# Gate and up projection of a decoder block as seven block products instead of eight, with the sums on VectorE

## What is computed

```python
h = rms_norm(x, norm_mix[l])
proj = h @ w_in[l]                                   # eight streams of 1024
# ... conv branch y_a, pooling branch y_p, cross-attention branch y_x ...
merged = sigmoid(g_a) * y_a + sigmoid(g_p) * y_p + sigmoid(g_x) * y_x
x = x + merged @ w_out[l]

h = rms_norm(x, norm_ffn[l])
x = x + (silu(h @ w_gate[l]) * (h @ w_up[l])) @ w_down[l]
return rms_norm(x, norm_final)
```

## Time and profile before

| | us |
|---|---|
| median of 3 runs | 1152.45 (1149.39 to 1160.99) |
| the profiled execution | 1155.09 |
| its span on the slowest core (core 0) | 1153.5 |
| spans of the other cores | 1144.2 to 1151.8 |
| busy in the span, TensorE / VectorE / ScalarE | 1117.5 / 475.7 / 305.2 |
| granted TensorE clock, mean of core 0 | 0.993 |

### The profile page before, as it was taken

The page is one execution under the profiler, slowest core; times in us unless marked ns, Lnnn a source line. Parts: engine busy times, 40 slices in busy tenths (PEclk is TensorE's granted clock), DMA queues, the critical chain, the costliest instruction groups (busy, mean ns, idle before and its releaser), DMA issues.

```text
span 1153.5 us, 14599 instructions; the slowest of 8 cores (1144.2 to 1153.5 us)
## 1 busy us (share of the span) xinstructions
PE 1117.5 (97%) x5472; PEld 543.1 (47%) x5574; DVE 475.7 (41%) x482; ACT 305.2 (26%) x490; POOL 79.0 (7%) x153
## 2 busy tenths in 40 slices
PE   7998999997999999999999999999999999999998
PEld 3665545553444444444444444444444444444444
DVE  5452555462765654654554632111324221112223
ACT  5432443423212224331212210111522121111111
POOL 1110000100011010001001000211000000000000
PEclk9998999999999999999999999999999999999999
DMA  9999861478387979345226453999966354200132
GB/s 246 173 205 203 148 128 55 80 159 127 74 137 209 258 164 175 67 123 110 56 54 110 74 146 110 204 182 171 172 164 194 101 117 82 40 1 1 37 110 110
DMA packets 78916, 146.34 MB, mean 127 GB/s; under 512 B 46571, under 2 KB 46571, under 8 KB 78592
## 3 DMA queue, kind: packets, MB, share of 16 engines
q0 software_dynamic: 21456, 77.64, 39.6%
q1 hardware_dynamic: 57392, 67.78, 20.2%
HBM read 185.27 MB, written 23.07 MB: 181 GB/s over the span
## 4 chain that ended last, share of the span: by engine, by line
PE 85%; DMA 10%; DVE 2%; issue 2%; ACT 1%; SPq 0%; DVEq 0%; ACTq 0%; POOLq 0%
PE ps L228 85%; DMA ring<-w_in 3%; DMA ring<-w_kv 3%; DMA arena<-hb 3%; DMA arena<-x 1%; ACT tmp L419 1%; DVE tmp L390 0%; SPq L177 0%; DVE tmp L470 0%; DVE smx L416 0%; DVE tmp L383 0%; DVE arena L397 0%; ACT tmp L387 0%; DVE tmp L483 0%; DVE hb L331 0%
## 5 line engine op out<-in xcount | busy, mean ns | idle before, releaser
L228 PE MATMUL ps<-hA,ring 128*128 128x512 bf16 (+3 forms) x2446 | 503.5, 363 | 6.6 <-ACT hA L352 2.5
L228 PEld LDWEIGHTS ps<-hA,ring 128*128 128x128 bf16 x2496 | 243.2, 98 | 259.6 <-issue 5.2
L228 PE MATMUL ps<-arena,ring 128*128 128x512 bf16 (+1 forms) x1575 | 333.3, 369 | 13.1 <-ACT tmp L460 6.1
L228 PEld LDWEIGHTS ps<-arena,ring 128*128 128x128 bf16 x1600 | 158.0, 99 | 184.2 <-issue 14.7
L228 PE MATMUL ps<-arena 128*128 128x512 bf16 (+1 forms) x838 | 180.4, 373 | 0.8
L629 DVE TENSOR_TENSOR arena<-ps,tmp 128x1024 bf16<-128x1024 f32 x44 | 53.9, 1225 | 227.9 <-PE ps L228 224.1
L228 PEld LDWEIGHTS ps<-arena 128*128 128x128 bf16 x854 | 83.6, 98 | 96.3
L625 ACT ACTIVATE tmp<-ps 128x1024 f32<-128x1024 f32 x44 | 45.0, 1023 | 253.4 <-PE ps L228 253.4
L470 DVE TENSOR_TENSOR tmp<-tmp 128x1024 f32<-128x1024 f32 (+6 forms) x40 | 49.2, 1230 | 41.4 <-ACT tmp L460 38.9
L228 PE MATMUL ps<-ring,arena 128*128 128x512 bf16 x250 | 57.4, 379 | 0.6 <-issue 0.2
L218 POOL DMA_DIRECT2D ring<-w_in x48 | 25.6, 538 | 440.0 <-PE ps L228 359.3
(11 more groups left out here) (98 smaller groups left out, 583.6 us busy)
## 6 DMA issues: line engine op xcount, KB each, us to landing
ring<-w_in POOLq DMA_DIRECT2D x48, 512.0 KB, 12.9
ring<-w_gate_up POOLq DMA_DIRECT2D x44, 512.0 KB, 12.2
arena<-x SPq DMA_DIRECT2D x32, 512.0 KB, 6.7
tmp<-x_scr SPq DMA_DIRECT2D x24, 512.0 KB, 5.3
x_scr<-arena SPq DMA_DIRECT2D x16, 512.0 KB, 3.5
out<-tmp SPq DMA_DIRECT2D x15, 512.0 KB, 3.3
arena<-w_down POOLq DMA_DIRECT2D x11, 512.0 KB, 24.3
ring<-w_kv POOLq DMA_DIRECT2D x8, 512.0 KB, 23.1
```

Source lines behind the costliest of these rows:

```text
L228: ins = e.matmul(o, l, r, start=s0, stop=s1)
```

## The change

**The scheme.** For a chunk the gate and up weights are a 2 by 2 block matrix (gate or up; first or second half of the contraction), and so are the tokens (half of the contraction; tokens 0 to 511 or 512 to 1023). The four output blocks come from seven products of four 128x512 matmuls each. For this some products need sums of weight blocks or of token blocks, and the outputs are sums of products.

**Token sums** (`x_sums`): for each of four blocks of 128 tokens five VectorE operations of 512 bf16 columns, into three ring slots that are taken for good (`x_slots`, `slots_held`) and in place in `HA`. For half 0 they are put into merge chunks 4 and 5 of half 1, for half 1 into the down stage of half 0. **Weight sums** (`w_sums`): for each chunk three VectorE operations in bf16, of 1024, 512 and 1024 columns, into `kT` or `vT` (free by then) and in place in the weight's slot. They are issued for chunk `c + 1` in the middle of chunk `c`; for chunk 0 in merge chunk 7, and at the last down tile of half 0.

**The chunk** (`gate_up`): three banks a chunk (A, C, D in the order bA, bC, bD). Bank D and bank A are written, read by VectorE and written again within the chunk; bank D and C also collect two products. The evaluation is 2 copies and 2 silus of 512 columns on ScalarE, and on VectorE two of 512, one of 1024 over two banks with one operand repeated, one of 512, and the product of 1024, now from two fp32 SBUF tiles, which is held back (`late`) into the next chunk.

**Order.** Out tiles of half 1 come after chunks 2 to 5 instead of within chunks 0 to 3. The first two gate-up loads are issued in merge chunk 6, the `w_out` loads after the first four of gate-up. The norms for `ffn(1)` all move to the down stage of half 0, two a tile in tiles 1 to 4, with their loads.

```diff
+    def x_sums(p):
+        ...
+        tt(dst("11+22"), x11, x22, ALU.add, lo + hi, [xq["11+22"].key()])
+        tt(dst("11+12"), x11, x12, ALU.add, lo, [xq["11+12"].key()])
+        n2 = dst("21+22")
+        dve(lambda e: e.scalar_tensor_tensor(out=n2, in0=x21, scalar=-1.0, in1=x22, op0=ALU.mult, op1=ALU.subtract),
+            hi, [xq["21+22"].key()])
+        tt(x12, x12, x22, ALU.subtract, lo + hi, lo)
+        tt(x21, x21, x11, ALU.subtract, lo + hi, hi)
+    ...
+    def w_sums(c, s):
+        ...
+        dve(lambda e: e.tensor_tensor(out=e_[:, 0:1024], in0=pairs[:, 0, :], in1=pairs[:, 1, :], op=ALU.add), sk, ek)
+        dve(lambda e: e.tensor_tensor(out=e_[:, 1024:1536], in0=w11, in1=w22, op=ALU.add), sk, [("wA", c % 2)])
+        dve(lambda e: e.tensor_tensor(out=mid, in0=quads[:, 0:4:2, :], in1=quads[:, 1:4:2, :], op=ALU.subtract), sk, sk)
+    ...
+    def gate_up(c, s, Q, between):
+        ...
+        prod(bC, ws_(512), xh(1, 1), True)
+        cp(T4[:, L], bC, ks)
+        prod(bD, ws_(1536), xs_("11+12"), True)
+        tt(T4[:, R], bank(bD), T4[:, L], ALU.add, kB(bD, 1) + ks, kt)
+        prod(bA, we(1024, wa), xs_("11+22"), True)
+        tt(T5[:, L], bank(bA), T4[:, R], ALU.subtract, kB(bA, 1) + kt, k5)
+        prod(bD, ws_(1024), xh(0, 0), False)
+        cp(T1[:, L], bD, k1)
+        while late:
+            late.pop(0)()
+        between()
+        prod(bA, we(512, ek), xh(0, 1), True)
+        prod(bC, ws_(0), xs_("21+22"), False)
+        cp(T2[:, R], bC, k2r, AF.Silu, -1.0)
+        two = T5[:, L].unsqueeze(1).broadcast_to((P, 2, 512))
+        o2 = T3[:, 0:1024].rearrange("p (a b) -> p a b", a=2)
+        ac = bank(bA, 2).rearrange("p (a b) -> p a b", a=2)
+        tt(o2, ac, two, ALU.add, kB(bA, 2) + k5 + k2r, k3)
+        act(lambda e: e.activation(out=T2[:, L], in_=T3[:, L], func=AF.Silu), k3, k2l)
+        prod(bD, we(0, ek), xh(1, 0), False)
+        tt(T1[:, R], bank(bD), T3[:, R], ALU.add, k3 + kB(bD, 1), k1)
+        late.append(lambda: tt(actT[:, c, :], T1[:, 0:TM], T2[:, 0:TM], ALU.mult, k1 + k2l + k2r, kA(c)))
 ...
     def s_hook(j, pos):
         s_tail()
+        if j in (4, 5) and pos == 2:
+            if j == 4:
+                x_slots()
+            x_sums(2 * (j - 4))
+            x_sums(2 * (j - 4) + 1)
+        if j == 6 and pos == 0:
+            gu0.extend(slot_load(w_gu_d[c]) for c in range(2))
+        if j == 7 and pos == 2:
+            w_sums(0, gu0[0])
 ...
-            gu_g(c, gu[c])
-            o1(hf, 2 * c)
-            gu_u(c, gu[c])
-            o1(hf, 2 * c + 1)
-            if hf == 0 and NF - 8 <= c < NF - 5:
-                cq.append(x1_load(1, c - NF + 8))
-            ...
+            gate_up(c, gu[c], r[:3] + r[3 + 2 * (c % 2):5 + 2 * (c % 2)],
+                    lambda: c + 1 < NF and w_sums(c + 1, gu[c + 1]))
+            if c >= 2:
+                o1(hf, 2 * c - 4)
+                o1(hf, 2 * c - 3)
+            if c + 4 < NF:
+                gu.append(slot_load(w_gu_d[c + 4]))
+        ...
+        ydq = [x1_load(hf, 0)]
+        if hf == 0:
+            cq = [(x1_load(1, t), t) for t in CO[0:2]]
         for i in range(NT):
             b = banks(2)
+            if hf == 0:
+                for p in cx:
+                    x_sums(p)
+                ...
+                if 1 <= i <= 4:
+                    for q2, t in cq:
+                        cp.append((Norm(T[q2][:, 0:D], [("T", q2)]).finish(), t))
+                    cq = [(x1_load(1, t), t) for t in CO[2 * i:2 * i + 2]]
+                if i == 1:
+                    gu0.extend(slot_load(w_gu_d[c]) for c in range(4))
+                if i == NT - 1:
+                    w_sums(0, gu0[0])
```

More of the change, by code:

```diff
@@ L621, in c_trans @@
         dma_transpose(b, HA[:, :, TOK0 + i * P:TOK0 + (i + 1) * P], [("HA", i + 1)])
[L623 to L630, removed]
+    xq = {}
@@ new lines, in build_program, with xs_, xh, ws_ @@
+    late = []
+    def gate_up(c, s, Q, between):
+        e_, ek, wa = wx[c % 2], wxk[c % 2], [("wA", c % 2)]
+        q4, q5, q3, q1, q2 = Q
+        T4, T5, T3, T1, T2 = [T[q] for q in Q]
+        k5, k3, k1 = [("T", q5)], [("T", q3)], [("T", q1)]
+        ks, kt, k2l, k2r = [("T", q4)], [("q4r", q4)], [("T", q2)], [("q2r", q2)]
+        lo, hi = [("HA", t) for t in range(1, 5)], [("HA", t) for t in range(5, 9)]
+        bA = banks(3)
+        bC, bD = bA + 1, bA + 2
+        def xs_(n):
+            return (lambda k: ring[:, xq[n].key()[1], k * 512:(k + 1) * 512]), [xq[n].key()]
+        def xh(tk, kh):
+            return (lambda k: HA[:, kh * 4 + k, TOK0 + tk * 512:TOK0 + (tk + 1) * 512]), (hi if tk else lo)
+        def ws_(o):
+            return (lambda k: rg(s, o + k * P, o + (k + 1) * P)), [s.key()]
+        def we(o, keys):
+            return (lambda k: e_[:, o + k * P:o + (k + 1) * P]), keys
+        def prod(b, w, x, first):
+            mms = [(bank(b), w[0](k), x[0](k), first and k == 0, k == 3) for k in range(4)]
+            def fn(e):
+                ins = None
+                for (o, l, r, s0, s1) in mms:
+                    ins = e.matmul(o, l, r, start=s0, stop=s1, skip_group_check=True)
+                return ins
+            plan.op("pe", fn, reads=w[1] + x[1], writes=kB(b, 1))
+        def cp(o, b, wr, fn=AF.Copy, sc=1.0):
+            act(lambda e: e.activation(out=o, in_=bank(b), func=fn, scale=sc), kB(b, 1), wr)
+        def tt(o, i0, i1, op, rd, wr):
+            dve(lambda e: e.tensor_tensor(out=o, in0=i0, in1=i1, op=op), rd, wr)
+        L, R = slice(0, 512), slice(512, 1024)
+        prod(bC, ws_(512), xh(1, 1), True)
[20 more added lines that the diff above has]
+        late.append(lambda: tt(actT[:, c, :], T1[:, 0:TM], T2[:, 0:TM], ALU.mult, k1 + k2l + k2r, kA(c)))
@@ L918, in build_program @@
     merge(1, H1, None)
-    sO = [slot_load(w_out_d[q]) for q in range(4)]
+    sO = []
     for i in range(3):
@@ L944, in build_program @@
     LASTB = ((0, 512), (512, 256), (768, 256))
+    CO = (0, 4, 1, 5, 2, 6, 3, 7)
     def ffn(hf):
[L947 to L948 removed]
+        gu = list(gu0)
+        while len(gu) < 4:
+            gu.append(slot_load(w_gu_d[len(gu)]))
+        gu0.clear()
+        if hf == 0:
+            sO.extend(slot_load(w_out_d[q]) for q in range(4))
         for c in range(NF):
[L950 to L951 removed]
             if hf == 0 and c in WD:
```

56 lines of the change are left out of this document (37 added, 19 removed).

## The result

| | before | after |
|---|---|---|
| median of 20 executions each, us | 1150.41 | 1161.43 |
| fastest, us | 1148.00 | 1158.96 |
| profiled execution, us | 1155.09 | 1167.43 |
| its span, us (slowest core) | 1153.5 (core 0) | 1165.9 (core 2) |
| gate-up of half 0, us | 179.58 | 184.8 |

The account below looks back on a forecast made before the run. The prediction took TensorE's matmuls to bound the kernel, moving to a VectorE and ScalarE chain. Half 0 -2.6 and half 1 +0.4 us sum to -2.2: 1155.1 to 1152.9 profiled, median 1150, range 1136 to 1180.

Parts of the forecast that it names:

- its likeliest case: The forecast's own sum of terms, chance 0.57; a time within about 1% counts as the same, chance 0.58.
- half 0: stage start to A: Entry of half 0's gate-up: weight sums and the last merge unit's two VectorE operations come first, 4.53 us.
- A: The first addition of a gate-up chunk, which reads the second product; an interval, A to A, was forecast at 6.83 us.
- first two intervals: First two chunks of a gate-up stage, taken as plain ones of 6.83 us each; 13.66 us in half 0.
- four intervals with out tiles: Chunks 2 to 5 of half 0, where TensorE sets the pace: 13.02 us each, 52.1 in all.
- fifteen plain intervals: The rest of half 0's gate-up, set by a VectorE and ScalarE chain: 6.83 us each, 102.5 in all.
- half 1: stage start to A: Entry of half 1's gate-up: VectorE still has the last down tile's add and scaling, 4.67 us.
- rival (b): In the weight sums: bf16 additions run at the fp32 rate, 1.34 us more an interval, +51, 1201 us; chance 0.07.
- Rival (a): Handoffs in the chunk's chain cost more, five steps without overlap: 0.9 us an interval, +35, 1185 us; chance 0.18.
- Rival (c): In the chunk, ScalarE doesn't delay A and VectorE alone sets 6.20 us: -24, 1126 us; chance 0.14.
- The other loops are shorter: Within a chunk: VectorE alone 6.20 us, TensorE 6.11, through the weight sums 6.33, all under the chain's 6.83.
- Rival (d): In gate-up TensorE, busy 88%, gets a lower clock: at 0.83 a chunk needs 7.3 us, +18, 1168 us; chance 0.04.

Follow-up runs that it names:

- the experiment with the copy first: Against the changed kernel, the silu of the joined addition's result is issued behind the next chunk's first copy; 1144.16 and 1143.61 us.
- the last kernel: Changed kernel with entries mended, weight sums before the late product, silus behind the next first copy (before out tiles in half 0's chunks 2 to 5); 1126.18 us, ratio 0.9778.
- the kernel with mended entries: Changed kernel with earlier first weight sums in half 0, the last down tile's scaling behind half 1's first two additions, and an early silu table load; ratio 1.0039.

## Where the prediction was right and where wrong

It said 1150 us, and the kernel takes 1161.43. The time lies in the range, and the change is under 1% as its likeliest case had it; but it is a loss, well clear of its interval, where a gain of 0.2% was forecast, and the miss of 11 us has a cause to be found. In the profiled execution the forecast was 1152.9 and the time 1167.43. Its terms against those measured on the slowest core:

| term | forecast, us | measured, us | difference |
|---|---|---|---|
| half 0: stage start to A | 4.53 | 5.75 | +1.2 |
| first two intervals | 13.7 | 16.9 | +3.2 |
| four intervals with out tiles | 52.1 | 52.9 | +0.8 |
| fifteen plain intervals | 102.5 | 105.0 | +2.5 |
| last A to the end | 4.28 | 4.25 | 0 |
| half 1: stage start to A | 4.67 | 4.61 | -0.1 |
| first two intervals | 13.7 | 16.9 | +3.2 |
| nineteen plain intervals | 129.8 | 133.3 | +3.5 |
| last A to the end | 4.28 | 4.25 | 0 |

Together +14.5 (from unrounded values); with the -2.2 of the forecast that is +12.3, which is 1167.4 - 1155.1.

**What held.** The bound moved from TensorE to a chain through VectorE and ScalarE. Every price of an operation held: 0.69, 1.22, 0.60, 0.63, and 0.68 and 0.42 for the bf16 sums, so rival (b) is out. The moved work and the token sums cost nothing, though the cover was counted wrong: a merge chunk is six units (gates p and x are two), 96 matmuls and 20.72 us, not five with 80 and 17.3. TensorE's busy share in the steady part reads 91% and not 88%, as the profile counts each product to the end of its last matmul; by turns it is 6.04 of 7.00 us, 86%. Rival (a)'s mechanism is out too: behind a finished wait the next VectorE operation still starts 0.08 us before the end (late product to sums 1.13, sums 0.60 and 0.53). Rival (c) could not be had as the program orders it, as the forecast argued; the experiment with the copy first and the last one are that rival made to happen.

**First failed step: the list of loops.** "The other loops are shorter" left one out. The joined addition has the silu from PSUM among its waits (the product it reads and that silu's share a bank, and the kernel keeps the two engines apart). With the forecast's own prices this path is A 0.69 + 0.14, three products 2.59, 0.10, silu 0.60, 0.10: 4.22 us, only 0.06 under the 4.28 through VectorE. A margin of 0.06 does not outlast the handoffs: measured, a last matmul ends 0.17 beyond its turn, ScalarE starts 0.09 after that, and the joined addition 0.17 after the silu, so 0.83 + 2.59 + 0.17 + 0.09 + 0.60 + 0.17 = 4.45. VectorE's own path came to 4.34. Interval 7.00 for 6.83, over 34 intervals +6.0 us; some 0.04 of it lies behind the joined addition, where A starts 0.16 after the copy for 0.10.

That the path through the silu sets the rest is shown by the kernel without weight sums (same interval, VectorE idle), by the 0.22 that came of 0.34, and by the last kernel, where the wait for the silu is gone and the joined addition comes 4.34 after A. Taking away that one wait and nothing else was not tried: the two engines would read one bank at once. The Trainium skill ("PSUM — Partial Sum Buffer", "PSUM bank collisions raise a hardware error") says that two engines must not touch one bank at the same time, reads too. No run here shows the error; the rule names the wait that the forecast overlooked.

A further branch was left out too. Product 5 waits for the subtraction, which reads its bank: 0.86 + 0.69 + 0.15 = 1.70 after A, and TensorE's own turn is 0.83 + 0.86 = 1.69 after it (the row at 1004.17). It is a tie, so the first stretch of the path may go by either, and no run parts them.

**Second failed step: the entries.** The forecast priced the late A and took every interval as a plain one. Two things lie in the first two. The silu's table: 1.28 us in each half, in front of the silu for which the joined addition waits; 8.31 - 7.0 in half 1. Before the change TensorE ran ahead over it. The Trainium skill ("ScalarE: Activation LUTs", "What ACT_TABLE_LOAD costs") gives 1283 ns for the load; the trace agrees. The same section of the Trainium skill adds some 1380 ns of drain to every switch. Nothing of that shows here: the silu starts at 934.53, 0.01 us after the load's end.

The second is the clock: after waits of 2.0 to 2.1 us the windows from 680 and from 938 above were granted 0.57 and 0.67, most of that time at 1.2 GHz instead of 2.4, with 16 and 8 matmuls spaced 0.43 us for 0.216 at these two entries on this core: 0.216 each is 3.5 and 1.7 us. The 16 are of two falls, each behind a wait of 2.05 us (before the products at 666.42 and at 679.26). In half 1 of this trace the fall is behind the second wait (2.12 us, before the product at 938.73) and not behind the first (2.68). The first of these falls makes the A of half 0 late: it starts at 669.95, when product 2, begun at 667.86, has taken 1.91 us for 1.03. Rival (d) had the mechanism in the wrong place: not the busy share of the steady part, which keeps its 1.00 at 91%, but the waits at the entries, which the forecast priced at their length alone. The kernel with mended entries shows both: 8.6 us off the stages of a core, first intervals at the plain length. How the table and the clock share the loss was not tried apart: a wait for the table is itself ahead of the second fall of the clock. The 1.3 and 1.7 us of half 1 are read from its timeline.

**A small one: the out tiles.** 13.22 us for 13.02. The last matmul's end (0.17) and the 0.09 after it, counted as 0.10, give 0.16 of the 0.20.

The median is 6 us below the profiled execution, whose slowest core spans 1165.9 us where the others span 1154.0 to 1160.9. The trace shows where: core 2 alone has the wait of 5.4 us for ScalarE in the merge of half 0, and it enters the gate-up stage at 664.2 us, the others at 653.9 to 658.9. Core 0 of the kernel before had such a wait too, so the two profiled executions compare like with like; why it comes is open. Against the median the miss is 11.4.

## What to carry to other kernels

When a change moves the bound from an engine's sum to a chain, list every wait of every operation in the new loop and price each path to it; two paths within 0.1 us of each other are one, and the later is set by handoffs that a sum tends to round down. Look at what stands in an in-order queue ahead of the next iteration's first operation: here a silu whose result no one needed for 2 us held back a copy that all waited for, and moving it alone gave 0.37 of the 0.65 us a chunk by which the best version beats the changed kernel. Price the first turns of a loop by themselves: a table load, and a stall after which the clock falls, each cost as much in half 1 as seven to ten turns of the error in the steady part.

## What the runs showed of the hardware

- A matmul of 512 columns takes its turn every 0.216 us, but the last of a product ends 0.17 us beyond its turn, and that counts only for a reader: four take 1.03 us to their end for 0.863 to the next product. The profile models these ends; what the start of the reader shows is the sum of 0.17 and the 0.09 below, 0.26 us.
- Handoffs from the end of one operation to the start of the next: TensorE to ScalarE 0.09 us, ScalarE to VectorE 0.16 to 0.23, VectorE to ScalarE 0.10, VectorE to TensorE 0.14. From A to the subtraction it was 0.17 in place of the 0.10 of the earlier trace rows, and that operation waits for a product too; whether the second wait makes the 0.07 was only argued.
- Joining two additions in one of 1024 columns over two banks, with one operand read twice by a broadcast, takes 1.22 us, as one plain addition of that width.
- bf16 additions in SBUF: 0.68 us for 1024 columns and 0.42 for 512, in place and over two strided blocks too. The token sums had one of another kind: a `scalar_tensor_tensor` of 512 bf16 columns in SBUF took 0.68 us (mean of 8), where the `tensor_tensor` of the same size took 0.42.
